# A 128-key weight matrix spilled to DRAM in groups of eight keys instead of four

## What is computed

```python
def _peer(h, w_pq, sub_keys, u_tab, v_tab):          # 512 tokens, D = 1024
    q = (xt @ w_pq).reshape(PEER_BLOCK, PEER_HEADS, 2, PEER_HALF)
    s = jnp.einsum('thpd,hpkd->thpk', q, sub_keys)   # two scores for each of 128 keys
    v1, i1 = lax.top_k(s[:, :, 0], PEER_TOPK)
    v2, i2 = lax.top_k(s[:, :, 1], PEER_TOPK)
    ...                                              # top 16 of the 256 sums v1 + v2
    eidx = ...                                       # i1 * 128 + i2
    g = jax.nn.softmax(top, axis=-1)
    a = jax.nn.gelu(jnp.einsum('thkd,td->thk', u_tab[eidx], xt))
    return jnp.einsum('thk,thkd->td', g * a, v_tab[eidx])
```

## Time and profile before

| | |
|---|---|
| median of 3 runs | 3872.63 us (3869.42 to 3872.78) |
| the profiled execution | 3872.8 us, of which 3871.1 us are the span from its first to its last instruction |
| PE busy | 3582.0 us, 93% of the span |
| DVE, ACT, POOL busy | 64%, 39%, 26% |
| granted clock of PE | 0.983 of full speed, mean |
| moved by DMA | 909.67 MB, mean 235 GB/s |

### The profile page before, as it was taken

The page is one execution under the profiler, slowest core; times in us unless marked ns, Lnnn a source line. Parts: engine busy times, 40 slices in busy tenths (PEclk is TensorE's granted clock), DMA queues, the critical chain, the costliest instruction groups (busy, mean ns, idle before and its releaser), DMA issues.

```text
span 3871.1 us, 54026 instructions
## 1 busy us (share of the span) xinstructions
PE 3582.0 (93%) x18308; PEld 2977.4 (77%) x18308; DVE 2483.5 (64%) x4635; ACT 1524.4 (39%) x2536; POOL 1018.9 (26%) x1283
## 2 busy tenths in 40 slices
PE   6999999998888799999989999999988788999998
PEld 4777699997777787777767777999977777877775
DVE  7455688887666675545464565888866667755554
ACT  3333233335666433322233333333366672323232
POOL 0000000014333533444300010000333336344442
PEclk8999999999999899999999999999999999999999
DMA  7443344448777998999744432444677779899995
GB/s 242 146 150 109 137 147 144 145 162 284 253 257 255 357 326 323 345 353 345 290 138 155 143 138 96 150 152 149 220 260 256 255 258 372 311 339 353 347 348 192
DMA packets 249073, 909.67 MB, mean 235 GB/s; under 512 B 32240, under 2 KB 32288, under 8 KB 248000
## 3 DMA queue, kind: packets, MB, share of 16 engines
q0 software_dynamic: 142912, 523.78, 38.2%
q1 hardware_dynamic: 105984, 383.83, 29.0%
HBM read 792.14 MB, written 115.34 MB: 234 GB/s over the span
## 4 chain that ended last, share of the span: by engine, by line
PE 71%; ACT 14%; DVE 9%; DMA 3%; issue 2%; POOL 1%; ACTq 0%; SPq 0%; DVEq 0%; POOLq 0%
PE ps L454 11%; PE ps L456 10%; PE ps L455 10%; PE ps L960 9%; PE ps L962 9%; PE ps L961 9%; ACT hotg L1169 5%; ACT stage L1193 4%; DVE whl L441 3%; PE ps L974 3%; DVE hotg L1588 3%; ACT whl L431 2%; DMA expert_spill<-hst 2%; PE ps L780 2%; PE ps L856 1%
## 5 line engine op out<-in xcount | busy, mean ns | idle before, releaser
L454 PE MATMUL ps<-mov,whl 128*128 128x384 f32 (+1 forms) x2880 | 1049.0, 364 | 72.8 <-DVE whl L441 28.7
L441 DVE TENSOR_TENSOR whl<-raw,whl 128x1024 fp32r<-128x1024 f32 x648 | 793.7, 1225 | 496.6 <-ACT whl L431 492.6
L456 PE MATMUL ps<-mov,whl 128*128 128x384 f32 (+1 forms) x2880 | 1018.3, 354 | 0.0
L455 PE MATMUL ps<-mov,whl 128*128 128x384 f32 (+1 forms) x2880 | 1017.8, 353 | 0.0
L431 ACT CAST whl<-raw 128x1024 fp32r<-128x1024 f32 x648 | 679.0, 1048 | 28.5 <-DMA raw<-in_w_in 28.4
L454 PEld LDWEIGHTS ps<-mov,whl 128*128 128x128 f32 x2880 | 546.9, 190 | 133.8 <-issue 43.8
L960 PE MATMUL ps<-whl,wgthl 128*128 128x512 f32 x1536 | 617.7, 402 | 20.1 <-DVE wgthl L1633 20.1
L962 PE MATMUL ps<-whl,wgthl 128*128 128x512 f32 x1536 | 610.7, 398 | 0.0
L961 PE MATMUL ps<-whl,wgthl 128*128 128x512 f32 x1536 | 610.0, 397 | 0.0
L456 PEld LDWEIGHTS ps<-mov,whl 128*128 128x128 f32 x2880 | 546.0, 190 | 35.4
L455 PEld LDWEIGHTS ps<-mov,whl 128*128 128x128 f32 x2880 | 547.7, 190 | 31.6 <-issue 2.4
(11 more groups left out here) (240 smaller groups left out, 3995.7 us busy)
## 6 DMA issues: line engine op xcount, KB each, us to landing
raw<-in_uT_tab SPq DMA_DIRECT2D x256, 512.0 KB, 4.2
raw<-in_v_tab SPq DMA_DIRECT2D x256, 512.0 KB, 5.9
expert_spill<-hst POOLq DMA_DIRECT2D x256, 192.0 KB, 2.2
weight_spill<-stage POOLq DMA_DIRECT2D x24, 2048.0 KB, 12.5
hin<-expert_spill POOLq DMA_DIRECT2D x256, 192.0 KB, 5.6
gt<-weight_spill POOLq DMA_DIRECT2D x64, 768.0 KB, 7.1
raw<-in_w_in SPq DMA_DIRECT2D x72, 512.0 KB, 4.5
raw<-in_w_mod SPq DMA_DIRECT2D x64, 512.0 KB, 3.6
```

Source lines behind the costliest of these rows:

```text
L441: nc.vector.tensor_tensor(whl[:, m % RING, 1], raw[:, raw_n(m) % RAW], whl[:, m % RING, 0].bitcast(F32), ALU.subtract).then_inc(lo_done, 1)
L454: nc.tensor.matmul(o, w[:, 0, k], src[:, 0, k, :cols], start=(k == 0), stop=False)
L455: nc.tensor.matmul(o, w[:, 0, k], src[:, 1, k, :cols], start=False, stop=False)
L456: mm = nc.tensor.matmul(o, w[:, 1, k], src[:, 0, k, :cols], start=False, stop=(k == KC - 1))
```

## The change

`AG` goes from 4 to 8. Nothing else is different in what is computed. In the program this means:

- The store of `stage` (24 of 2 MB) writes, for each of the 128 partitions, 16 runs of 1 KB instead of 32 runs of 512 bytes.
- The load of `gt` takes 1536 KB instead of 768 KB, and there are 16 a layer instead of 32. A partition reads 12 KB in one run instead of 6 KB. The two loads of the second bridge are both of the large size.
- The load of a later group is issued after every eighth key instead of after every fourth.
- The two `gt` buffers grow from 12 KB to 24 KB for each partition. They move to where `stage` lies. `otok`, which takes the sums at the end of the layer, now shares their place, and ACT waits for the last weight product (`w_ready`) before it writes there.
- DVE reads `gt` with a step of 1 KB from one block of 32 tokens to the next, instead of 512 bytes.

```diff
-AG = 4
+AG = 8
...
-    gt = sb("gt", [P, 2, NTB, AG, TB], at=hot_at)
...
-    otok = sb("otok", [P, TT, D])
     e32 = sb("e32", [P, QUADS, QUADS])
-    assert top_of[0] <= hot_at
+    otok = sb("otok", [P, TT, D], at=top_of[0])
+    gt = sb("gt", [P, 2, NTB, AG, TB])
+    assert top_of[0] <= nc.sbuf_usable_end
...
+            act.wait_ge(w_ready, l * P + P)
             for half in range(2):
                 for t in (2, 0):
...
-                dve.wait_ge(gt_in[j // 4 % 2], l * (2 * P) + 16 * (j // 8 + 1))
+                dve.wait_ge(gt_in[j // AG % 2], l * (8 * P // AG) + 16 * (j // (2 * AG) + 1))
...
-                                        gt[:, j // 4 % 2, :, j % 4], ALU.mult).then_inc(w_made, 1)
+                                        gt[:, j // AG % 2, :, j % AG], ALU.mult).then_inc(w_made, 1)
```

## The result

The changed kernel took 3878.32 us (median of 18 runs, 3875.24 to 3881.8) against 3872.91 us for the kernel before, run beside it (median of 18). Two of those eighteen runs took 5981.5 and 6798.38 us, and the ratio leaves them out. The ratio is 1.0015, with a 95% interval of 1.0008 to 1.0022. The change makes the kernel 5.4 us slower, clear of noise but within the 0.2% that the prediction called "same". It had forecast 3878.6 us.

A forecast was written before the change was run, and what follows sets the result against it. PE was taken to bound the kernel, its idle time set in the bridges by `hst` stores behind large transfers on POOL's full queue. 7.6 - 2.6 + 1.0 = 6.0 us later gave 3878.6 us, own range 3873.2 to 3887.0.

The forecast's parts named there:

- same: Whole kernel: a time of 3864.9 to 3880.4 us, which runs can't tell from before; chance 0.54.
- What bounds: Second bridge: PE's gaps follow two `hst` stores; each microsecond of DMA work added ahead of them costs one at the end.
- Part 2: Second bridge: two larger `gt` loads delay the second `hst` store by 3.8 us (3.4 to 5.2), 7.6 us in both layers.
- Part 1: Second bridge: the twelfth `stage` store in 1 KB runs saves 1.3 us a layer (0 to 3.2), 2.6 in all.
- Part 3: Stage 5 around key 24: a larger `gt` load delays `hin`, 0.6 us first layer, 0.4 second, together 1.0 us.
- The sum: Whole kernel: loads 7.6, store -2.6 and key 24 1.0 make 6.0 us later, 3878.6 us; chance 0.50.
- A: Bridge: 1 KB runs lose the whole 3.2 us surcharge, key 24 finds room; +1.2 us, 3874 us; chance 0.15.
- B: Store of `stage`: gains nothing, its surcharge being that of writing to DRAM; +8.6 us, 3881 us; chance 0.15.
- C: Bridge: first PE gap shrinks to 2.6 us, PE keeps 2.4 GHz, second `hst` store undelayed; -10.4 us, 3862 us; chance 0.08.
- D: Rest of stage 5: `hin` late at four keys a layer, 1 to 1.9 us each; about 3890 us; chance 0.12.

The follow-up runs named there:

- the loads alone: Kernel before with four `gt` buffers and four loads of 768 KB in the second bridge instead of two, stores still in runs of 512 bytes: ratio 1.0016.
- the store alone: Kernel before with stores of `stage` in runs of 1 KB, loads still 768 KB but reading runs of 512 bytes: ratio 1.0002.

## Why the prediction was right

**What bounds.** Right. The two bridges grew by 5.5 us, and the medians differ by 5.4 us. PE waits at the two places named, and stage 3 and the rest of stage 5 hardly matter. The conclusion that a microsecond of DMA work ahead of these stores is a microsecond of the end is right only roughly: single steps in the experiments were worth from 0.6 to 1.7 times their bytes at 415 GB/s.

**Part 2, the loads.** Right in mechanism, and a little too large. 3.8 us were worked out, and the second critical store does take 3.81 us more in the first layer and 3.75 in the second. But this store is also issued sooner after the last one-hot product, into the same backlog, and so waits longer. What counts is the bridge. With the loads alone it is 3.2 us a layer longer, just below the low bound of 3.4.

**Part 1, the store.** Right in place and sign, mis-sized. The term of 1.3 us a layer measured 0.6 us. That half of the surcharge goes is borne out by the rates in the bridge (an estimated 2.1 us before, 0.9 after). The step that failed is to carry this over to the landing in full: the first critical store was to take 11.4 us and takes 12.65, `weight_spill` was to land 1 to 3 us sooner and lands 0.4 us sooner, and the first gap was to be 4.5 us and is 5.24. That this store lands 0.6 us sooner goes with its issue, which comes 0.5 us sooner, about what POOL saves in issuing the store of `stage` (1762 to 1229 ns). The prediction had counted nothing for that. The rule of the Trainium skill ("DMA: Bandwidth & Descriptors", specifications) makes this term 0, about as far from 0.6 us as the 1.3 us of the forecast. But 512 bytes aren't at the full rate here: while DMA is busy it moves 349 GB/s with runs of 512 bytes and 382 and 393 with 1 KB and 16 KB.

**Part 3, key 24.** The term of 1.0 us is about 0.2 us: PE's gap grew from 0.53 to 0.70 us, in the first layer alone. Most of the added bytes cost nothing there, and no run shows why.

**The sum.** With the measured sizes it is 6.4 - 1.2 + 0.2 = 5.4 us, in the place of 7.6 - 2.6 + 1.0 = 6.0. Three errors, of -1.2 us in the loads, +1.4 in the store and -0.8 at key 24, largely cancel. That the forecast of 3878.6 us meets 3878.32 us so closely is in part luck.

**The rivals.** A needed the whole surcharge to go; even runs of 16 KB don't do that, and the bridge stays at +3.5 us. B is refuted by the first gap of the kernel with the store alone, 4.89 against 5.84 us, though 0 was no worse a price for the store than 1.3. C needed a first gap of some 2.6 us, and it is 3.46 us with the longest runs. D didn't happen: no gap after key 32. The longest landing of `hin` from 1480 to 1900 us rose from 10.7 us to 13.1 us, just short of the 15 us at which it would:

```profile
DMA to landing us min/median/max: 3.4/6.0/13.1
```

## What to carry to other kernels

Cost a larger transfer by what stands behind it on its queue, at the moment at which the queue is full, and not by its mean landing time: 22 of the 24 better stores and 28 of the 32 larger loads were worth next to nothing, and four loads decided the result. The same loads behind the store that is waited for made the bridges 9.1 us shorter. Before the granularity of a spill is changed, look at which piece of it is really needed at the hand-over between two stages. Deferring the second piece past the start of stage 5 made either group size faster than the original (0.9988 and 0.9989), and moving eight gathers out of the full stretch into one with room gave three times as much (0.9964).

## What was not expected of the hardware

A load from DRAM in runs of 512 bytes took longer too. The median landing of a 768 KB load rose from 7.1 to 8.1 us when each partition's 6 KB went from one run to twelve of 512 bytes. POOL's issue of the load rose with it, from 542 to 1037 ns, and may be half of the difference. The tile view of `gt` in the kernel with the store alone:

```profile
L660 POOL DMA_DIRECT2D gt<-weight_spill x64: 1035/1037/1081, 1307.2 to 3797.6; - x64
...
DMA to landing us min/median/max: 6.5/8.1/15.0
```

POOL's time to issue a store rises with the number of its runs: 1762 ns with 4096 runs, 1229 ns with 2048, and in the kernel with runs of 16 KB and 128 of them:

```profile
L698 POOL DMA_DIRECT2D weight_spill<-stage x12: 575/576/585, 935.3 to 1282.8; - x12
```

These three don't lie on one line (0.26 us for each thousand runs between 2048 and 4096, 0.34 below), but a store of many short runs holds POOL up for over a microsecond.
